# Eight additional tokens on fetched rows in place of sixteen, with low parts taken one product later and early row picks moved ahead of the scatter

## The chip, the cores and the metric

One core of one Trainium2 chip runs the whole program. The metric is device time in microseconds (us) of one launch. The kernel before took 2079.82 us in the median of three runs (2076.31 to 2084.03).

## The reference, cut to what matters

The program is two transformer blocks over 512 tokens of width 1024. The first block has attention and a convolution, then a mixture of 16,384 tiny experts ("PEER"); the second has sparse attention and a recurrence. The change touches the expert layer only:

```
s = einsum('chpd,hpnd->chpn', q, keys)       # 8 heads, two halves, 128 keys each
sv, si = top_k(s, 16)                        # per head and half
top_s, sel = top_k(sv0[:, None] + sv1[None, :], 16)
eidx = si0 * 128 + si1 at sel                # 8 x 16 = 128 experts for a token
g = softmax(top_s)
act = gelu(einsum('chkd,cd->chk', u_tab[eidx], xb))
out = einsum('chk,chkd->cd', g * act, v_tab[eidx])
```

So each token uses 128 rows of `u_tab` and 128 rows of `v_tab`, 1024 floats each.

## The kernel before, in words

**Two ways through the experts.** The first FETCH = 128 tokens take the reference's way: each sits on a partition, and an indirect DMA fetches one row per token, 512 KB a fetch, 128 fetches from u and 128 from v. The next EXTRA = 16 tokens take it too, laid out as 16 tokens by SHARED = 8 rows a fetch, so 16 fetches of u and 16 of v. For each fetched tile VectorE does one multiply with a sum (u) or one multiply and add (v) over 128x1024: a "pick". The other 512 - 128 - 16 = 368 tokens go densely: all 16,384 experts are multiplied with them, `gelu(u x)` is multiplied with a gate that is zero for experts not chosen, and the result is multiplied with v. `REST - EXTRA` = 368 is the number of columns of each of these matmuls.

**The dense way.** Every fp32 product is made of three fp32r matmuls: high weights with high data, high weights with low data, low weights with high data (L515 to L517, and L921 to L923). A weight tile is 128x1024 (512 KB), and gives 8 x 3 = 24 matmuls. For each tile SP starts the load `wraw` (ring of 4), ScalarE casts it to the high part `wh` (ring of 3), and GpSimd, or for every other tile VectorE, subtracts to get the low part `wl`. There are 16 groups of 8 tiles of u and 8 of v. The u products of nine groups ("spilled", 72 tiles) are made early, during routing, and their gelu is stored in DRAM (`a_scratch`); the u products of the seven others (56 tiles) are made in the expert loop, and all 128 v products too.

**Routing and scatter.** `drive_routing` is an order written out by hand that all engines follow. Routing of 128 tokens at a time is a chain of VectorE sorting steps. In its first two rounds the spilled products run beside it. Then three rounds of 128 tokens each turn the chosen gates into dense gate matrices: for four tokens (a "quad") VectorE builds one-hot tiles (`hots`), ScalarE weighs them, TensorE multiplies them. During these loops VectorE makes the first EARLY_PICKS = 42 picks, from three row buffers. GpSimd's `pick` issues the fetches: at its pick number m it issues rows up to m + 3, and waits for the pick that frees the buffer, all in order with its `wl` work.

**The expert loop** goes U(n+1, i+1), V(n, i), U(n+1, i+2), V(n, i+1) and so on. For U(n, i) VectorE multiplies gelu with the gate (L2421), ScalarE casts that to its high part WTH (L1652), VectorE waits for the cast and subtracts for WTL (L2424). For V(n, i) VectorE makes `wl` when it is its turn, waits for the product, adds it to h (L2436), and makes its picks. `fetch_schedule` deals the picks that are left (251) over the products. ScalarE casts the next weight tile in the same order as its WTH casts. Where the next group is spilled, no u product stands between two v products ("crowded" below); where it isn't, the loop is called "dense".

SP's queue holds the loads of weights, of gates, and of spilled tiles; before it loads a spilled tile it waits until WTH and WTL have been made from the tile five places earlier (L2985 to L2989).

Of the kernel before, what the change touches and what calls it, by code (L numbers as in the profile page):

```python
# [45 lines left out]
BLOCKS = REST // 32  # L46
EXTRA = 16
SHARED = 128 // EXTRA
# [94 lines left out]
def build_program(nc, hT, wstream, gains, consts, trig, w_uq, w_ukv, keys, w_uk, w_uv, w_rg, u_rows, v_rows, out):  # L143
# [1137 lines left out]
    def drive_routing(route, spill, spilled, scatter, pick, ahead=None):  # L1281

        for tt in range(2):
            steps = route(tt)
            for n in range(13):
                for _ in range(2):
                    next(steps, None)
                spill()
                if tt == 1 and n > 2:
                    pick()  # L1290
                if tt == 1 and n % 3 == 2:
                    spill()
            for _ in steps:
                pass
        picks = 10
        for tt in range(1, 4):
# [3 lines left out]
            for n in range(begin, 16):  # L1300
# [11 lines left out]
                scatter((tt - 1) * 128 + n * 8)  # L1312
                while picks < (10, 18, 26)[tt - 1] + (8, 8, 16)[tt - 1] * now // whole:
                    pick()
                    picks += 1
                while done < ROUTE_STEPS * now // (whole - 1):
                    next(steps, None)
                    done += 1
# [566 lines left out]
    def vector(dve):  # L1885
# [511 lines left out]
        def picks_after():  # L2397
            for _ in range(PICKS_AT[product_no[0]]):
                pick()
            product_no[0] += 1  # L2400


        dve.tensor_tensor(gg, gn[:, GCOL["g_fin"]:GCOL["g_fin"] + 8], gn[:, GCOL["g2"]:GCOL["g2"] + 8],
                          ALU.mult).then_inc(*scaled.tell("gg"))
        for what, n, i in EXPERTS:
            if what == "U":
# [14 lines left out]
                dve.tensor_tensor(u, u, gr[n % 2][:, :, i * 32:i * 32 + 32], ALU.mult).then_inc(*gated.tell((n, i)))  # L2421
                for x in ([i - 1] if n == 0 and 0 < i else []) + ([i] if n > 0 or i == 7 else []):
                    dve.wait_ge(*wt_hi.at(n, x))
# [8 lines left out]
            if n == N_GROUPS - 1 and i > 1:  # L2432
# [3 lines left out]
            dve.tensor_tensor(hx[i][:, FETCH + EXTRA:S], bank_of["V", n, i][:, EXTRA:REST], hx[i][:, FETCH + EXTRA:S],  # L2436
                              ALU.add).then_inc(*h_added.tell(("V", n, i)))
            picks_after()
            if (n, i) == (N_GROUPS - 2, 7):
# [260 lines left out]
    def gpsimd(pool):  # L2700
# [135 lines left out]
        def pick():  # L2836
            made[0] += 1
            fetch(min(made[0] + 3, EARLY_PICKS))

# [297 lines left out]
```

## Time and profile before

| what | us |
|---|---|
| median of three runs | 2079.82 |
| profiled execution, its own time | 2077.86 |
| its span in the trace | 2075.9 |
| TensorE matmul busy | 2025.1 |
| VectorE busy | 1475.7 |
| GpSimd busy | 1061.3 |
| ScalarE busy | 997.2 |

The page's first part gives busy time of each engine; matmuls are pipelined, and their recorded lengths overlap, so that two matmuls whose starts are 0.167 us apart each show 0.33 us. The rate of starts (the x of a stretch) tells more than the busy share. In the 40 slices VectorE stands at 8 or 9 tenths from about 830 us to 1450 us, and the DMA engines at 9 from about 730 us to 1450 us.

### The profile page before, as it was taken

Reading aid. Unit: us, or ns where it says so; the run is one execution under the profiler, and the core shown is the slowest. Engines: PE = TensorE matmul, PEld = TensorE weight load, DVE = VectorE, ACT = ScalarE, POOL = GpSimd, SP = SyncE. Lnnn points to the kernel's source line nnn. Section 1 sums busy time; section 2 is a strip of 40 time slices with the busy share of each in tenths; the row PEclk is TensorE's granted clock in tenths of the full one; section 3 lists DMA queues with packets and bytes.
Section 4 is the critical chain, followed back from the end, with each engine's and each line's share of the span. In section 5 each row is a group of like instructions: output and inputs, shape, how many; then the busy total and the mean of one; then the engine's idle time right before and its main releaser. Section 6 shows DMA issues by size and latency. Waiting matters only on the chain.

```text
span 2075.9 us, 31764 instructions
## 1 busy us (share of the span) xinstructions
PE 2025.1 (98%) x11815; PEld 1804.4 (87%) x11815; DVE 1475.7 (71%) x2840; ACT 997.2 (48%) x1825; POOL 1061.3 (51%) x615
## 2 busy tenths in 40 slices
PE   9999999999999999999999999999999999999998
PEld 8746889999999999999999999999967777877777
DVE  6247547979999478888888888887687535067763
ACT  4347433367789733333333333333546652356643
POOL 3222456864446577685667767684344444411242
PEclk9999999999999999999999999999999999999999
DMA  5330225776669899999999999996322223210021
GB/s 203 80 99 12 82 82 173 253 240 229 239 236 325 311 338 372 362 391 356 328 374 344 367 336 396 336 388 244 120 77 76 84 91 111 95 41 31 21 82 61
DMA packets 150935, 435.31 MB, mean 210 GB/s; under 512 B 14464, under 2 KB 61184, under 8 KB 148992
## 3 DMA queue, kind: packets, MB, share of 16 engines
q1 hardware_dynamic: 109312, 282.29, 39.1%
q0 software_dynamic: 41472, 151.01, 19.3%
q8 instruction: 95, 1.56, 0.3%
q14 instruction: 56, 0.46, 0.1%
HBM read 391.28 MB, written 41.97 MB: 209 GB/s over the span
## 4 chain that ended last, share of the span: by engine, by line
PE 76%; DVE 12%; DMA 4%; issue 4%; ACT 3%; POOL 2%; SPq 0%; DVEq 0%; ACTq 0%
PE bank L515 15%; PE bank L516 14%; PE bank L517 14%; PE bank L921 4%; PE bank L922 4%; PE bank L923 4%; DMA wraw<-in_wstream 4%; PE bank L902 3%; DVE wide L2390 2%; PE bank L1142 2%; PE bank L690 1%; DVE wl L1917 1%; DVE fetched L2370 1%; ACT WTH L1652 1%; POOL fetched L2830 1%
## 5 line engine op out<-in xcount | busy, mean ns | idle before, releaser
L2704 POOL TENSOR_TENSOR wl<-wraw,wh 128x1024 fp32r<-128x1024 f32 x272 | 678.8, 2500 | 716.7 <-ACT wh L1330 714.2
L1330 ACT CAST wh<-wraw 128x1024 fp32r<-128x1024 f32 x360 | 375.8, 1047 | 173.3 <-PE bank L517 118.3
L515 PE MATMUL bank<-WTH,wh 128*128 128x368 f32 x1024 | 340.4, 332 | 22.2 <-ACT wh L1330 11.3
L515 PE MATMUL bank<-XH,wh 128*128 128x368 f32 (+2 forms) x976 | 344.7, 353 | 3.0 <-issue 1.9
L516 PE MATMUL bank<-XL,wh 128*128 128x368 f32 (+2 forms) x976 | 340.8, 349 | 0.0
L517 PE MATMUL bank<-XH,wl 128*128 128x368 f32 (+2 forms) x976 | 339.5, 348 | 0.0
L516 PE MATMUL bank<-WTL,wh 128*128 128x368 f32 x1024 | 337.4, 330 | 0.0
L517 PE MATMUL bank<-WTH,wl 128*128 128x368 f32 x1024 | 337.2, 329 | 0.0
L515 PEld LDWEIGHTS bank<-WTH,wh 128*128 128x128 f32 x1024 | 192.8, 188 | 32.1 <-ACT wh L1330 21.4
L515 PEld LDWEIGHTS bank<-XH,wh 128*128 128x128 f32 x976 | 183.4, 188 | 25.7 <-issue 7.3
L921 PE MATMUL bank<-XH,wh 128*128 128x368 f32 x576 | 196.3, 341 | 7.1 <-ACT ijgT L1574 2.6
L516 PEld LDWEIGHTS bank<-XL,wh 128*128 128x128 f32 x976 | 183.2, 188 | 18.5 <-issue 2.2
L517 PEld LDWEIGHTS bank<-XH,wl 128*128 128x128 f32 x976 | 183.5, 188 | 16.4
L2830 POOL DMA_INDIRECT fetched<-in_u_rows,diag x144 | 158.0, 1097 | 69.0 <-DVE fetched L2370 41.2
L517 PEld LDWEIGHTS bank<-WTH,wl 128*128 128x128 f32 x1024 | 192.9, 188 | 0.0
L516 PEld LDWEIGHTS bank<-WTL,wh 128*128 128x128 f32 x1024 | 192.8, 188 | 0.0
L922 PE MATMUL bank<-XL,wh 128*128 128x368 f32 x576 | 191.7, 333 | 0.0
L923 PE MATMUL bank<-XH,wl 128*128 128x368 f32 x576 | 191.1, 332 | 0.0
L2830 POOL DMA_INDIRECT fetched<-in_v_rows,diag x144 | 161.5, 1122 | 42.9 <-issue 26.9
L2390 DVE SCALAR_TENSOR_TENSOR wide<-fetched,diag,wide 128x1024 f32<-128x1024 f32 x127 | 163.0, 1283 | 10.7 <-DMA fetched<-in_v_rows,diag 7.0
L1917 DVE TENSOR_TENSOR wl<-wraw,wh 128x1024 fp32r<-128x1024 f32 (+1 forms) x92 | 114.5, 1245 | 6.1 <-ACT wh L1330 5.2
L1652 ACT CAST WTH<-tmp 128x368 fp32r<-128x368 f32 x72 | 36.1, 501 | 171.8 <-DVE tmp L2421 149.2
(552 smaller groups left out, 3903.1 us busy)
## 6 DMA issues: line engine op xcount, KB each, us to landing
wraw<-in_wstream SPq DMA_DIRECT2D x360, 512.0 KB
g_scratch<-gs SPq DMA_DIRECT2D x12, 2048.0 KB
gr<-g_scratch SPq DMA_DIRECT2D x15, 1536.0 KB
a_scratch<-tmp SPq DMA_DIRECT2D x72, 184.0 KB
tmp<-a_scratch SPq DMA_DIRECT2D x46, 184.0 KB
sq<-a_scratch SPq DMA_DIRECT2D x26, 184.0 KB
shifted<-hc_scratch SPq DMA_DIRECT2D x12, 270.0 KB, 4.8
fetched<-in_u_rows,diag POOLq DMA_INDIRECT x144
```

The costliest lines, as they stand in the source:

```text
L515: pe.matmul(o, w1, x1, start=n == 0, stop=False)
L516: pe.matmul(o, w1, x2, start=False, stop=False)
L517: m = pe.matmul(o, w2, x1, start=False, stop=n == len(ks) - 1)
L902: mm = pe.matmul(bank[:, i * 128:i * 128 + 128], hots[q % 4][1][:, i, :], hots[q % 4][0][:, i, :], start=True, stop=True, skip_group_check ...
L921: pe.matmul(o, w1s[:, c:c + 128], XH[:, k, FETCH + EXTRA:S], start=k == 0, stop=False)
L922: pe.matmul(o, w1s[:, c:c + 128], XL[:, k, FETCH + EXTRA:S], start=False, stop=False)
L923: mm = pe.matmul(o, w2s[:, c:c + 128], XH[:, k, FETCH + EXTRA:S], start=False, stop=k == KT - 1)
L1330: act.copy(wh[n % NSPLIT][:, :], wraw[n % NRAW][:, :]).then_inc(*w_hi.tell(n))
L1917: return dve.tensor_tensor(lo, src, hi.bitcast(F32), ALU.subtract)
L2390: dve.scalar_tensor_tensor(wide[1][:, :], flat, eweight[:, s:s + 1], wide[1][:, :], ALU.mult, ALU.add).then_inc(*picked.tell(("v", s)))
L2704: return pool.tensor_tensor(lo, src, hi.bitcast(F32), ALU.subtract)
L2830: pool.indirect_dma_start(fetched[buf][:, :], None, u_rows if what in ("u", "u2") else v_rows, bass.IndirectOffsetOnAxis(ap=(eidx if what ...
```

## The change

EXTRA goes from 16 to 8 (SHARED from 8 to 16), so the dense matmuls have 376 columns in place of 368, there are 8 fetches less of u and 8 less of v, and the scatter has two quads more. VectorE's subtraction for WTL of groups 1 to 15 moves from U(n, i) to behind the addition to h of V(n-1, i-1) (both of the first two behind V(n-1, 0)). In the second routing round 14 picks are made in place of 10; the next two rounds of the scatter have 6 each in place of 8. Fetches are issued up to row m + 2 in place of m + 3. Routing steps beside the scatter end one iteration sooner.

```diff
--- before.py
+++ after.py
@@ -44,7 +44,7 @@
 FETCH = 128
 REST = S - FETCH
 BLOCKS = REST // 32
-EXTRA = 16
+EXTRA = 8
 SHARED = 128 // EXTRA
 EARLY_PICKS, LEAD, NEARLY, NFETCH = 42, 4, 3, 6
 NCAND = 80
@@ -1286,13 +1286,15 @@
                 for _ in range(2):
                     next(steps, None)
                 spill()
-                if tt == 1 and n > 2:
+                if tt == 1 and n > 1:
                     pick()
+                    if n in (8, 10, 12):
+                        pick()
                 if tt == 1 and n % 3 == 2:
                     spill()
             for _ in steps:
                 pass
-        picks = 10
+        picks = 14
         for tt in range(1, 4):
             steps = route(tt + 1) if tt < 3 else iter(())
             done = 0
@@ -1310,10 +1312,10 @@
                 if ahead:
                     ahead(KT * base + KT * count * now // whole)
                 scatter((tt - 1) * 128 + n * 8)
-                while picks < (10, 18, 26)[tt - 1] + (8, 8, 16)[tt - 1] * now // whole:
+                while picks < (14, 20, 26)[tt - 1] + (6, 6, 16)[tt - 1] * now // whole:
                     pick()
                     picks += 1
-                while done < ROUTE_STEPS * now // (whole - 1):
+                while done < min(ROUTE_STEPS, ROUTE_STEPS * now // (whole - 2)):
                     next(steps, None)
                     done += 1
 
@@ -2402,6 +2404,11 @@
 
         dve.tensor_tensor(gg, gn[:, GCOL["g_fin"]:GCOL["g_fin"] + 8], gn[:, GCOL["g2"]:GCOL["g2"] + 8],
                           ALU.mult).then_inc(*scaled.tell("gg"))
+        def low_part(n, x):
+            dve.wait_ge(*wt_hi.at(n, x))
+            minus_high(WTL[n % 2][:, x, EXTRA:], active(n, x)[:, EXTRA:],
+                       WTH[n % 2][:, x, EXTRA:]).then_inc(*wt_lo.tell((n, x)))
+
         for what, n, i in EXPERTS:
             if what == "U":
                 j = U_AT[n, i]
@@ -2419,7 +2426,7 @@
                 if n == 0 and i == 4:
                     dve.wait_ge(*ld_g[2].at("rest"))
                 dve.tensor_tensor(u, u, gr[n % 2][:, :, i * 32:i * 32 + 32], ALU.mult).then_inc(*gated.tell((n, i)))
-                for x in ([i - 1] if n == 0 and 0 < i else []) + ([i] if n > 0 or i == 7 else []):
+                for x in ([i - 1] if n == 0 and 0 < i else []) + ([i] if n == 0 and i == 7 else []):
                     dve.wait_ge(*wt_hi.at(n, x))
                     minus_high(WTL[n % 2][:, x, EXTRA:], active(n, x)[:, EXTRA:],
                                WTH[n % 2][:, x, EXTRA:]).then_inc(*wt_lo.tell((n, x)))
@@ -2435,6 +2442,9 @@
             dve.wait_ge(*gemm.at("V", n, i))
             dve.tensor_tensor(hx[i][:, FETCH + EXTRA:S], bank_of["V", n, i][:, EXTRA:REST], hx[i][:, FETCH + EXTRA:S],
                               ALU.add).then_inc(*h_added.tell(("V", n, i)))
+            if n + 1 < N_GROUPS:
+                for x in (0, 1) if i == 0 else (i + 1,) if i < 7 else ():
+                    low_part(n + 1, x)
             picks_after()
             if (n, i) == (N_GROUPS - 2, 7):
                 dve.wait_ge(*row_sum_mm.at("all"))
@@ -2835,7 +2845,7 @@
 
         def pick():
             made[0] += 1
-            fetch(min(made[0] + 3, EARLY_PICKS))
+            fetch(min(made[0] + 2, EARLY_PICKS))
 
         drive_routing(route, spill, spilled, scatter, pick)
 
```

## Rows read from the trace of the kernel before

**Rows 1.** The page, first part: busy time of each engine.

```profile
PE 2025.1 (98%) x11815; PEld 1804.4 (87%) x11815; DVE 1475.7 (71%) x2840; ACT 997.2 (48%) x1825; POOL 1061.3 (51%) x615
```

**Rows 2.** Windows: stretch, length, busy (count) of each engine, clock, DMA share, GB/s.

```profile
300.00:425.00 125.00, 123.81 (x767) 121.65 (x766) 102.46 (x446) 49.86 (x68) 91.52 (x41) 1.00 0.63 206
425.00:530.00 105.00, 98.19 (x648) 96.17 (x647) 92.61 (x267) 73.42 (x177) 52.77 (x27) 0.97 0.67 225
...
725.00:1430.00 705.00, 680.95 (x4019) 670.62 (x4018) 597.15 (x788) 248.18 (x340) 490.26 (x330) 1.00 0.97 360
```

**Rows 3.** The same view: the crowded stretches, last but one and the sum.

```profile
1280.00:1345.00 65.00, 60.22 (x353) 58.36 (x353) 56.17 (x69) 21.82 (x30) 39.49 (x26) 1.00 0.96 355
...
sum 273.00, PE 254.86 PEld 247.90 DVE 232.62 ACT 95.97 POOL 162.89; mean PE 36.41 PEld 35.41 DVE 33.23 ACT 13.71 POOL 23.27
```

**Rows 4.** The same view: the dense stretches, the last and the sum.

```profile
1345.00:1414.00 69.00, 69.00 (x415) 69.00 (x414) 60.99 (x68) 25.45 (x34) 54.14 (x39) 1.00 1.00 377
sum 419.00, PE 413.09 PEld 409.72 DVE 359.85 ACT 146.50 POOL 317.37; mean PE 68.85 PEld 68.29 DVE 59.98 ACT 24.42 POOL 52.90
```

**Rows 5.** Groups by shape, TensorE: count, busy us, mean ns, idle before.

```profile
L516 PE MATMUL bank<-WTL,wh 128*128 128x368 f32 x1024 | 337.4, 330 | 0.0
...
L922 PE MATMUL bank<-XL,wh 128*128 128x368 f32 x576 | 191.7, 333 | 0.0
...
L516 PE MATMUL bank<-XL,wh 128*128 128x512 f32 x384 | 151.8, 395 | 0.0
...
L516 PE MATMUL bank<-XL,wh 128*128 128x368 f32 x448 | 148.1, 331 | 0.0
...
L516 PE MATMUL bank<-XL,wh 128*128 128x264 f32 x144 | 40.9, 284 | 0.0
```

**Rows 6.** Waits from 725 to 1430 us: who for whom, total, times, longest.

```profile
ACT WTH L1652 <- DVE tmp L2421: 144.3, 53, 7.5
...
DVE WTL L1917 <- ACT WTH L1652: 64.2, 106, 3.0
...
ACT wh L1330 <- DMA wraw<-in_wstream: 24.5, 13, 3.9
```

**Rows 7.** VectorE in order of time, two products of a crowded stretch.

```profile
1299.37 1.12 DVE L2421 TENSOR_TENSOR tmp<-tmp,gr 128x384 f32<-128x384 f32 x1
1301.06 0.54 DVE L1917 TENSOR_TENSOR WTL<-tmp,WTH 128x368 fp32r<-128x368 f32 x1 [0.57 <-ACT WTH L1652]
1301.97 1.28 DVE L2390 SCALAR_TENSOR_TENSOR wide<-fetched,diag,wide 128x1024 f32<-128x1024 f32 x1
...
1307.51 1.12 DVE L2421 TENSOR_TENSOR sq<-sq,gr 128x384 f32<-128x384 f32 x1
```

**Rows 8.** The chain that ended last, 1010 to 1032 us: its longest piece.

```profile
1014.10 15.26 DMA wraw<-in_wstream
```

**Rows 9.** Groups by shape, VectorE: later u picks, then the 42 early ones.

```profile
L2370 DVE SCALAR_TENSOR_TENSOR fetched<-fetched,wide 128x1024 f32<-128x1024 f32 x86 | 102.8, 1214 | 10.3 <-DMA fetched<-in_u_rows,diag 9.8 <-issue 0.5
L2370 DVE SCALAR_TENSOR_TENSOR fetched<-fetched,below_XH 128x1024 f32<-128x1024 f32 x42 | 73.3, 1748 | 3.7 <-DMA fetched<-in_u_rows,diag 3.7
```

**Rows 10.** VectorE in order of time, second routing round to first one-hot tiles.

```profile
390.41 1.82 DVE L2370 SCALAR_TENSOR_TENSOR fetched<-fetched,below_XH 128x1024 f32<-128x1024 f32 x1 [2.21 <-DMA fetched<-in_u_rows,diag]
...
412.06 3.43 DVE L2370 SCALAR_TENSOR_TENSOR fetched<-fetched,below_XH 128x1024 f32<-128x1024 f32 x1
...
432.44 2.36 DVE L2327 TENSOR_TENSOR hots<-wide,ijgT 128x1024 f32<-128x1024 f32 x2 [5.55 <-ACT ijgT L1574]
...
435.85 1.28 DVE L2317 TENSOR_TENSOR sq<-wide,ijgT 128x512 f32<-128x512 f32 x2
```

**Rows 11.** GpSimd in order of time, the same stretch.

```profile
383.19 0.97 POOL L2830 DMA_INDIRECT fetched<-in_u_rows,diag  x1
...
410.78 6.98 POOL L2704 TENSOR_TENSOR wl<-wraw,wh 128x1024 fp32r<-128x1024 f32 x2
```

**Rows 12.** The chain that ended last: the scatter's matmuls for two quads.

```profile
529.93 1.78 PE bank L902 x16
```

## The prediction

> **What bounds the kernel now.** I read the page's first part first: TensorE is busy 98% of the span, VectorE 71%, GpSimd 51% [rows 1]. That makes TensorE the bound on average, so work added to it is paid in full wherever it doesn't idle. The windows then show where it does idle [rows 2]: 1.2 us of the 125 in the second routing round, 6.8 of 105 at the start of the scatter, 24 of 705 in the expert loop, where the DMA share is 0.97. I split the expert loop into the stretches in which the next group is spilled (crowded, 273 us) and the others (dense, 419 us), because the work per product differs. Crowded, TensorE idles 273 - 254.9 = 18.1 us [rows 3]; dense, 419 - 413.1 = 5.9 us [rows 4]. The reader is to see the rate as well: the crowded row has 353 matmuls in 65 us (0.184 us each), the dense one 415 in 69 us (0.166).
>
> Who sets the crowded pace? VectorE in order of time [rows 7]: from 1299.37 to 1307.51 it makes two products' share in 8.14 us, with no idle time but two waits of 0.57 us for ScalarE's cast WTH. TensorE would need 48 x 0.1666 = 8.0 us for two products. That pair has one pick a product; the schedule deals 83 picks to 72 crowded products, 1.15 each, so the mean pair takes 8.14 + 0.3 x 1.28 = 8.5 us, 0.5 more than TensorE's, and 36 pairs give 18 us: the same as the idle time of rows 3. The waits view agrees: VectorE waits 64 us for WTH in 106 places, and ScalarE 144 us (and more for the tiles named sq) for VectorE's gate product [rows 6], behind which ScalarE's next weight cast is queued. So in the crowded stretches TensorE follows VectorE. In the dense ones what is left looks like DMA: in the chain a weight load takes 15.26 us, just after a group's gates were asked for [rows 8], and ScalarE waits 24.5 us for weights in 13 places [rows 6].
>
> **The change part by part.** Everything is set against the profiled execution, 2077.86 us (span 2075.9 and 2 around it); the median of the runs is 2 us above it.
>
> *Columns.* 56 x 24 dense u matmuls, 72 x 24 spilled, 128 x 24 of v are 6144 (rows 5 show one third of each: 448, 576, 1024). Mean lengths are 330 to 333 ns at 368 columns, 395 at 512, 284 at 264 [rows 5]; their ends are modelled, but the differences follow the starts. Slopes are (395 - 331) / 144 = 0.444 and (331 - 284) / 104 = 0.452 ns a column. Eight columns are 3.56 ns, and 6144 of them 21.9 us. From below, a column per cycle of the 2.4 GHz level (the granted clock is 1.00 in nearly all windows) gives 20.5. I take 21.9, all on the path, as TensorE is the bound.
>
> The Trainium skill (TensorE: Matmul & The Clock Gate, Back-to-back issue gap) puts a sustained stream with weight loads at about 81 ns for 128 columns and 131 for 512, that is 0.13 ns a column; by that the columns would cost 6.4 us in place of 21.9. The rows contradict it with their 0.44 to 0.45.
>
> *Two more quads in the scatter.* Their matmuls take 1.78 us [rows 12], on TensorE's path: +1.8. VectorE pays two one-hot products of about 1.2 for one quad and 1.28 in two halves for the other [rows 10], 2.5 us, which the two picks taken out of that round give back (below).
>
> *Sixteen fetches less.* 16 x 1.28 = 20 us less of VectorE, 16 of GpSimd's issues of about 1 us, 8.4 MB less of DMA traffic, which at the loop's 360 GB/s [rows 2] is 23 us of a 705 us stretch. None of it is on TensorE; it counts only by what waits for it.
>
> *Low parts one product later.* VectorE now finds the cast finished and loses the 0.57 us [rows 7]. Its crowded pair becomes 8.5 - 1.14 - 0.1 (picks 1.10 a product in place of 1.15) = 7.3 us against TensorE's 48 x 0.170 = 8.17: it stops being the bound. What is late next: with the dense stretches' share of idle time (5.9 / 419), 3.8 us of the 18.1 stay for DMA, 14.3 go; a restart costs more than the idle time shows (in the crowded row 65 - 353 x 0.1663 = 6.3 us lost for 4.8 idle), so 14.3 x 1.3 = 18.6. I take -18. Bounds: 0 if something else holds the pace, and all the loop's losses, 24 x 1.3 = 31, if the dense ones go too. The new place adds a wait on no engine's path, I think: SP loads a spilled tile only when WTL of five places earlier is there, and the weight load is queued behind it; but that weight load needs the low part of a tile whose cast starts after the same v product (1.05 + 2.4 us later), while WTL follows that product by an addition and a subtraction, 1.1 us. V(n+1, 0) needs WTL of tile 7 last; it is made behind V(n, 6), with V(n, 7)'s 4 us in between.
>
> *Fourteen early picks ahead of the scatter.* Four more picks at a mean of 1.75 us [rows 9] are 7 us of VectorE before the first one-hot tile. There VectorE idles 5.55 us for TensorE's transposed gates [rows 10], and TensorE arrives there 30 x 24 x 3.56 ns = 2.6 us later than now: 8.1 us of cover. But rows are fetched late as well: today's fetch at 383.19 [rows 11] feeds the pick at 390.41, which waited 2.21 us for it [rows 10], and the same row is now picked one iteration (some 5 us) sooner, the later ones fetched one iteration later relative to their use. Where GpSimd's subtraction runs beside a pick, the pick takes 3.43 us and not 1.2 [rows 10, 11]. So the cover may fail by a little: I take +1, between 0 (covered) and 4 x 3.43 + 4 x 2.21 - 8.1 = 14 us.
>
> The Trainium skill (SBUF — State Buffer, Who interferes with whom) says that a VectorE instruction with two SBUF inputs contends with a GpSimd instruction that reads SBUF. The 3.43 us beside GpSimd's 6.98 us pair agree with it; by that rule all four new picks could be long, 4 x 3.43 = 13.7 us and 5.6 beyond the cover.
>
> *Start of the scatter.* From 425 to 530 us TensorE idles 6.8 us and the clock fell twice (mean 0.97) while VectorE is full [rows 2]. VectorE's work there stays (two picks out, one pair of quads in), TensorE's grows by 15 spilled tiles x 24 x 3.56 ns + 1.8 = 3.1 us: it fills idle time, -3. Bounds 0 and -8 (idle time and clock).
>
> *Fetches one row later.* GpSimd is not held up by VectorE before a subtraction; in the last round the slack of a row shrinks from some 3 us, but VectorE is at 0.8 there. 0, with +5 as the upper bound, one iteration.
>
> Sum: +21.9 + 1.8 - 18 + 1 - 3 = +3.7, 2081.6 for a profiled execution, and 2 more for the median: 2083.
>
> **The rivals.** (A) *Relief everywhere.* Less traffic and a freer VectorE let weight loads start earlier, so the DMA waits of the dense stretches go too. For it: 8.4 MB less, and loads wait for VectorE's low parts. Against: the 15 us loads come with a group's gates, which stay. -31 in the loop, -8 at the scatter: 23.7 - 39 = -15, 2065. (B) *Relief nowhere*, slower: the crowded pace is held by ScalarE's weight casts queued behind WTH or by DMA at 0.97 of its share, and the low parts' wait only moves. It decides if the rate of crowded stretches stays at 0.18 us a matmul. For it: DMA share; against: VectorE without a gap [rows 7] and ScalarE busy 96 of 273 us [rows 3]. +23.7 and nothing back: 2104. (C) *The early picks delay the scatter*: rows land late, VectorE reaches the first one-hot tile 5 to 14 us after TensorE; it decides once the cover of 8.1 us is gone. 2083 + 9 = 2092. (D) *Columns are cheap*: the matmul's pitch grows by about 1 ns and not 3.56; 2083 - 15.5 = 2067. Against it stand both slopes of rows 5. The rule of the Trainium skill cited above (TensorE: Matmul & The Clock Gate) would bring this about.
>
> **How the numbers follow.** Forecast 0.61 (its own range 2074 to 2092), A 0.14, B 0.13, C 0.10, D 0.02. The interval that leaves out 2 in 10: 2068 to 2097. A measurement tells 0.5% from no change, 10.4 us. Faster than 2069.4: most of A, D and a little of the forecast, 0.15. Slower than 2090.2: B, most of C, and a little of the forecast, 0.22. Same 0.63.
>
> **What would show it.** Right: mean length of a 376-column matmul 3.5 ns longer; VectorE's wait for WTH from 64 us to under 10, crowded stretches at 0.171 to 0.173 us a matmul, and VectorE with idle time in them for TensorE's products; dense ones hardly changed but for the columns; first one-hot tile at 434 to 437 us. Wrong: crowded stretches still at 0.18 (B), dense idle gone (A), the first one-hot tile after 440 us (C), the same matmul lengths (D).

## The result and the profile after

The changed kernel took 2082.03 us (median of 20 runs, 2078.88 to 2085.28), the kernel before 2076.64 in as many runs beside it (2069.63 to 2084.28, and one of 5131.72). The ratio is 1.0024 [1.0014, 1.0035]: 5 us slower, within the 0.5% called the same. The predicted 2083 and its 0.63 for "same" hold, though the forecast stood on a kernel before of 2079.82, 3.2 us above the 2076.64 measured here: as a difference it said +3.2, and the ratio gives +5.0 [2.9, 7.3]. The profiled execution has a span of 2083.0 us against 2075.9, which is 7.1 us more. The total came out right, but two terms behind it did not: TensorE pays 35 us for the eight columns and not 22, and its pauses shrink by 28 us and not by 20.

The page, first part, as [rows 1]. TensorE has 1% more of a longer span and hardly pauses; VectorE is busier by 22 us although it makes 16 picks less (part of why stands below), GpSimd less by 26.

```profile
PE 2056.5 (99%) x11831; PEld 1843.2 (88%) x11831; DVE 1497.5 (72%) x2819; ACT 999.9 (48%) x1835; POOL 1035.8 (50%) x599
```

The windows that answer to [rows 2], cut where the same work now lies: second routing round, start of the scatter, expert loop. In the last one TensorE was busy 681 us of 705; now it is 701.5.

```profile
300.00:425.00 125.00, 123.81 (x748) 121.67 (x747) 102.20 (x442) 46.73 (x64) 88.87 (x40) 1.00 0.62 203
425.00:535.00 110.00, 105.61 (x694) 103.58 (x693) 101.31 (x275) 80.18 (x191) 55.69 (x29) 0.98 0.65 223
...
735.00:1440.00 705.00, 701.49 (x4051) 700.20 (x4050) 613.19 (x773) 251.84 (x345) 457.91 (x315) 1.00 0.96 349
```

The crowded stretches, last but one and the sum of the seven, against [rows 3]. Idle time fell from 18.1 to 3.5 us. The seven rows count 1526 matmuls in 267 us, 0.175 each; the seven of before count 1501 in 273, 0.182.

```profile
1283.00:1349.00 66.00, 62.90 (x360) 61.93 (x360) 61.96 (x70) 22.27 (x31) 40.10 (x27) 1.00 0.95 346
...
sum 267.00, PE 263.49 PEld 262.24 DVE 254.31 ACT 99.43 POOL 162.25; mean PE 37.64 PEld 37.46 DVE 36.33 ACT 14.20 POOL 23.18
```

The dense stretches against [rows 4]: TensorE has no idle time left, where it had 5.9 us.

```profile
1349.00:1419.00 70.00, 70.00 (x406) 70.00 (x405) 61.00 (x63) 23.96 (x32) 46.31 (x35) 1.00 0.98 354
sum 420.00, PE 420.00 PEld 419.97 DVE 349.75 ACT 145.47 POOL 283.61; mean PE 70.00 PEld 69.99 DVE 58.29 ACT 24.24 POOL 47.27
```

The waits from 735 to 1440 us, against [rows 6]. VectorE's wait for the cast WTH is 1.8 us and was 64; it now waits for TensorE's products (46.0 us). ScalarE's wait for weights fell from 24.5 to 8.0 us, its wait for the gate product only from 144 to 137.

```profile
ACT WTH L1654 <- DVE tmp L2428: 137.2, 62, 6.7
...
DVE h L2443 <- PE bank L517: 46.0, 45, 2.7
...
ACT wh L1332 <- DMA wraw<-in_wstream: 8.0, 7, 3.5
...
DVE WTL L1919 <- ACT WTH L1654: 1.8, 4, 0.5
```

VectorE in order of time in the same crowded stretch, against [rows 7]: the low part (WTL) follows the addition to h with 0.1 us between, without the 0.57 us.

```profile
1305.64 0.53 DVE L2443 TENSOR_TENSOR h<-bank,h 128x376 f32<-128x376 f32 x1
1306.29 0.55 DVE L1919 TENSOR_TENSOR WTL<-tmp,WTH 128x376 fp32r<-128x376 f32 x1
1306.76 1.28 DVE L2392 SCALAR_TENSOR_TENSOR wide<-fetched,diag,wide 128x1024 f32<-128x1024 f32 x1
```

Something the prediction didn't count: in its new place the subtraction for WTL is longer. The first line is the kernel before, the second the changed one; the mean of one goes from 731 to 875 ns.

```profile
L1917 DVE TENSOR_TENSOR WTL<-tmp,WTH 128x368 fp32r<-128x368 f32 x72 | 52.6, 731 | 41.2 <-ACT WTH L1652 37.2 <-issue 4.0
L1919 DVE TENSOR_TENSOR WTL<-tmp,WTH 128x376 fp32r<-128x376 f32 x72 | 62.7, 875 | 3.6 <-ACT WTH L1654 1.8
```

Counted over all 128 of these subtractions, 10 took over 0.6 us before and 52 after (46 in low_later, below), and all but one of the long ones overlap a subtraction of GpSimd, where 3 of 118 short ones did before and 26 of 76 after. Their sum goes from 86 to 107 us (130 in low_later). In low_at_once, which has the old place, it is 87 us, so it is the new place in VectorE's order and not the columns.

VectorE ahead of the scatter, against [rows 10]. Three picks run one behind the other from 432.00 to 440, the first of them in 5.76 us (GpSimd subtracts beside it from 431.92 to 436.67; all 20 of the 42 early picks that took over 1.4 us overlap such a subtraction), and the first one-hot tile (below_XL here) comes at 439.99; in the kernel before the one-hot tiles began at 432.44.

```profile
391.00 3.19 DVE L2372 SCALAR_TENSOR_TENSOR fetched<-fetched,below_XH 128x1024 f32<-128x1024 f32 x1 [4.37 <-DMA fetched<-in_u_rows,diag]
...
432.00 5.76 DVE L2372 SCALAR_TENSOR_TENSOR fetched<-fetched,below_XH 128x1024 f32<-128x1024 f32 x1 [1.06 <-DMA fetched<-in_u_rows,diag]
...
438.84 0.08 DVE L2372 DVE_READ_ACCUMULATOR fetched<-fetched,below_XH 128x1 f32 x1
438.84 1.21 DVE L2372 SCALAR_TENSOR_TENSOR fetched<-fetched,below_XH 128x1024 f32<-128x1024 f32 x1
439.99 0.08 DVE L2372 DVE_READ_ACCUMULATOR fetched<-fetched,below_XH 128x1 f32 x1
439.99 1.21 DVE L2329 TENSOR_TENSOR below_XL<-wide,ijgT 128x1024 f32<-128x1024 f32 x1
```

**Phases, worked out from the start of every matmul.** Each cell: length of the phase in us / sum of TensorE's pauses in it, a pause being a distance between two starts above 0.4 us, less 0.17. The other three columns are the mean distance of two starts within products (distances under 0.24 us), in ns.

| kernel | routing | scatter | expert loop | tail | spilled u | dense u | v |
|---|---|---|---|---|---|---|---|
| before | 130.3 / 1.1 | 266.4 / 9.1 | 775.8 / 29.2 | 596.9 | 167.9 | 167.9 | 166.8 |
| after | 135.6 / 2.6 | 270.3 / 5.1 | 772.7 / 4.0 | 598.2 | 172.8 | 173.2 | 173.2 |
| low_later | 130.3 / 1.1 | 266.2 / 9.2 | 756.1 / 13.4 | 597.5 | 167.9 | 167.9 | 166.7 |
| fetches_only | 130.3 / 1.1 | 265.8 / 8.7 | 763.2 / 17.9 | 596.9 | 167.8 | 167.9 | 166.8 |
| columns_only | 134.0 / 1.1 | 271.0 / 8.5 | 781.7 / 12.0 | 597.9 | 172.8 | 173.2 | 173.2 |
| columns_384 | 136.4 / 1.1 | 271.0 / 8.5 | 787.9 / 13.1 | 597.3 | 175.5 | 175.4 | 173.8 |
| low_at_once | 136.1 / 3.1 | 270.5 / 4.9 | 776.6 / 7.1 | 598.3 | | | |
| early_undone | 134.0 / 1.1 | 268.6 / 6.3 | 769.1 / 0.8 | 597.1 | 172.8 | 173.2 | 173.2 |
| early_only | 136.8 / 5.2 | 266.6 / 7.6 | 771.4 / 26.3 | 597.3 | | | |
| sixteen | 134.4 / 4.1 | 265.4 / 7.3 | 758.2 / 14.2 | 597.0 | | | |
| low_steps | 130.3 / 1.1 | 274.3 / 14.3 | 763.2 / 19.1 | 597.4 | 167.9 | 167.8 | 166.7 |
| placed | 134.7 / 2.8 | 269.7 / 6.0 | 763.1 / 0.9 | 597.3 | 171.3 | 168.3 | 173.3 |
| v_at_0 | 134.0 / 1.1 | 268.6 / 6.1 | 768.8 / 0.8 | 598.4 | 172.8 | 172.5 | 173.3 |

The loop's pauses, split into crowded and dense stretches by whether dense u products are under 10 us apart (crowded / dense, us): before 22.1 / 7.0, low_later 12.2 / 1.2, fetches_only 12.7 / 5.3, columns_only 10.8 / 1.2, after 4.0 / 0.0.

Each row is one execution. That of low_later is the fastest of its runs (2058.68 us, median 2063.28), that of low_steps the slowest (2073.00, median 2067.86), so a few us between such rows need not come from the edit.

### The profile page after: what moved, and what is told of

Same layout as the page of the kernel before. It is cut to its first block, busy times and chain, and to the rows that moved or that the text cites. A ratio compares the mean times of both kernels' runs of the same rounds, so it can differ in the third digit from the quotient of the medians.

```text
span 2083.0 us, 31764 instructions
## 1 busy us (share of the span) xinstructions
PE 2056.5 (99%) x11831; PEld 1843.2 (88%) x11831; DVE 1497.5 (72%) x2819; ACT 999.9 (48%) x1835; POOL 1035.8 (50%) x599
## 4 chain that ended last, share of the span: by engine, by line
PE 88%; DVE 7%; DMA 2%; issue 1%; POOL 1%; ACT 1%; SPq 0%; DVEq 0%; ACTq 0%
PE bank L515 19%; PE bank L516 19%; PE bank L517 19%; PE bank L921 4%; PE bank L922 4%; PE bank L923 4%; PE bank L902 3%; PE bank L1142 2%; PE bank L690 1%; DMA wraw<-in_wstream 1%; PE wide L1165 1%; PE wide L1153 1%; PE bank L1165 1%; PE wide L648 1%; PE bank L784 1%
## 5 line engine op out<-in xcount | busy, mean ns | idle before, releaser
L1332 ACT CAST wh<-wraw 128x1024 fp32r<-128x1024 f32 x360 | 375.9, 1045 | 209.3 <-PE bank L517 173.3
L515 PE MATMUL bank<-XH,wh 128*128 128x376 f32 (+2 forms) x976 | 347.1, 356 | 1.1 <-ACT wh L1332 1.0
L515 PE MATMUL bank<-WTH,wh 128*128 128x376 f32 x1024 | 343.3, 335 | 3.5 <-issue 3.5
L517 PE MATMUL bank<-WTH,wl 128*128 128x376 f32 x1024 | 343.1, 335 | 0.0
L516 PE MATMUL bank<-WTL,wh 128*128 128x376 f32 x1024 | 343.0, 335 | 0.0
L516 PE MATMUL bank<-XL,wh 128*128 128x376 f32 (+2 forms) x976 | 343.0, 351 | 0.0
L517 PE MATMUL bank<-XH,wl 128*128 128x376 f32 (+2 forms) x976 | 342.1, 351 | 0.0
L515 PEld LDWEIGHTS bank<-XH,wh 128*128 128x128 f32 x976 | 183.4, 188 | 23.3 <-issue 3.9
L921 PE MATMUL bank<-XH,wh 128*128 128x376 f32 x576 | 197.8, 343 | 2.5 <-issue 2.4
L922 PE MATMUL bank<-XL,wh 128*128 128x376 f32 x576 | 193.2, 335 | 0.0
L923 PE MATMUL bank<-XH,wl 128*128 128x376 f32 x576 | 192.7, 335 | 0.0
L921 PEld LDWEIGHTS bank<-XH,wh 128*128 128x128 f32 x576 | 108.3, 188 | 5.5 <-issue 4.5
```

The costliest lines, as they stand in the source:

```text
L515: pe.matmul(o, w1, x1, start=n == 0, stop=False)
L516: pe.matmul(o, w1, x2, start=False, stop=False)
L517: m = pe.matmul(o, w2, x1, start=False, stop=n == len(ks) - 1)
L921: pe.matmul(o, w1s[:, c:c + 128], XH[:, k, FETCH + EXTRA:S], start=k == 0, stop=False)
L922: pe.matmul(o, w1s[:, c:c + 128], XL[:, k, FETCH + EXTRA:S], start=False, stop=False)
L923: mm = pe.matmul(o, w2s[:, c:c + 128], XH[:, k, FETCH + EXTRA:S], start=False, stop=k == KT - 1)
```

## The experiments

Each ratio is to the kernel before, timed on the same chip. To compare them, 0.1% is 2.08 us.

**low_later**: the kernel before, with the low parts later and nothing else of the change.

```diff
-                for x in ([i - 1] if n == 0 and 0 < i else []) + ([i] if n > 0 or i == 7 else []):
+                for x in ([i - 1] if n == 0 and 0 < i else []) + ([i] if n == 0 and i == 7 else []):
...
+            if n + 1 < N_GROUPS:
+                for x in (0, 1) if i == 0 else (i + 1,) if i < 7 else ():
+                    low_part(n + 1, x)
```

> The kernel before with one part of the change alone: the low parts of groups 1 to 15 are taken behind the addition of the v product before. Sixteen additional tokens, picks and fetches as before. Theory 1 (VectorE held the pace of the crowded stretches by its waits for the cast): its pair of products falls from 8.5 to 7.4 us, under TensorE's 8.0, the wait of VectorE for WTH falls from 64 us to under 10, gaps in the expert loop fall from 29 us to under 8, time -20 us (2056). Rival B (ScalarE's casts or DMA hold the pace): the wait disappears, the gaps stay, time within 3 us of before.

Measured: 2063.28 us, 0.9947 [0.9928, 0.9966], that is -11 us [-15, -7]; in the profiled execution -19. Its waits (725 to 1430 us) and its expert loop:

```profile
ACT wh L1330 <- DMA wraw<-in_wstream: 29.1, 21, 2.9
...
DVE WTL L1917 <- ACT WTH L1652: 7.6, 10, 3.0
```

```profile
725.00:1411.00 686.00, 674.86 (x4022) 670.36 (x4021) 639.10 (x789) 247.88 (x342) 475.87 (x331) 1.00 0.99 370
```

The wait for the cast goes and half of the loop's pauses with it, in the crowded stretches (22.1 to 12.2 us) and in the dense ones (7.0 to 1.2); in the crowded ones the rows of six windows have 1421 matmuls in 245 us, 0.172 each. So that wait did hold TensorE. Theory 1 has its sign and not its size: pauses of 13.4 us and not under 8, -11 us and not -20. What stays is the wait for weights, longer than before (29.1 us against 24.5), at a DMA share of 0.99.

**columns_only**: the kernel before with 376 dense columns; the additional tokens' gates are zero there, so the eight columns add nothing to the output.

```diff
+FIRST = 8
-        later = lambda name, *freed: ([(FETCH + EXTRA, S)], [name], [freed])
-        weighted = lambda name, *freed: ([(EXTRA, REST)], [name], [freed])
+        later = lambda name, *freed: ([(FETCH + FIRST, S)], [name], [freed])
+        weighted = lambda name, *freed: ([(FIRST, REST)], [name], [freed])
```

> The kernel before with 376 columns in the dense matmuls (tokens 8 to 15 of the additional sixteen go the dense way too, with gates of zero) and nothing else: fetches, picks, scatter and low parts as before. Theory 1 with the pitch seen in the changed kernel (5 ns more a matmul, 6144 of them): +31 us, less what the crowded stretches absorb, where TensorE's pair grows from 8.0 to 8.24 us under VectorE's 8.5: 36 x 0.24 = 9; +22 us (2098), and mean length of one matmul 335 ns. By the slope of the prediction (3.56 ns): +22 - 6 = +16 us and 333.5 ns. By the rule of the Trainium skill (TensorE: Matmul & The Clock Gate, Back-to-back issue gap), 1 ns a matmul, it would be +6 us; nothing else rests on this sentence.

Measured: 2093.16 us, 1.0085 [1.0065, 1.0106]: +17.7 us. The starts lie 4.9 to 6.4 ns further apart, and not 3.56; over 1728 spilled, 1344 dense u and 3072 v matmuls that is 8.5 + 7.1 + 19.7 = 35.3 us. It doesn't all reach the span, since the slower products give others time: the loop's pauses fall from 29.2 to 12.0 us with no other edit, and ScalarE's wait for weights (725 to 1430 us) from 24.5 to 10.4, though the wait for the cast is as long as it was and the traffic is no smaller. So the wait for weights is in part a consequence of TensorE's pace. Of the expected times both +22 and +16 lie in the interval [+13.5, +22]; the distance of the starts is theory 1's or more.

```profile
DVE WTL L1918 <- ACT WTH L1653: 70.0, 115, 3.1
...
ACT wh L1331 <- DMA wraw<-in_wstream: 10.4, 9, 2.8
```

**fetches_only**: the kernel before with eight additional tokens in all that fetches and picks (two more quads with it), the dense products still at 368 columns; tokens 136 to 143 are left out of the expert layer.

```diff
-EXTRA = 16
+EXTRA = 8
+FIRST = 16
...
-        weighted = lambda name, *freed: ([(EXTRA, REST)], [name], [freed])
+        weighted = lambda name, *freed: ([(FIRST, REST)], [name], [freed])
```

> The kernel before with eight additional tokens instead of sixteen in everything that handles fetched rows and picks (two more quads of routed work, 16 picks and half of the additional columns of each row's copy fewer), while the dense matmuls keep their 368 columns; tokens 136 to 143 are left out of the expert layer. What the expert layer gives back for the columns is measured alone. Theory (work on VectorE and the fetches keep TensorE in the crowded loop; less of it is quicker): the last expert loop loses 3 to 8 us and the whole is 0.996 to 0.999 of before (2067 to 2073). Rival (two more quads cost as much as the smaller row copies give): within 0.1% of before. Rival two, from the run with sixteen tokens against the change's own (the expert layer with eight was not seen to be any quicker): slower, 1.001 or more.

Measured: 2063.44 us, 0.9945 [0.9929, 0.9962], -11.4 us: more than the theory expected and against both rivals, and the clearest contradiction of the prediction, which gave the sixteen fetches nothing of their own. The first of the rows is the start of the scatter, where TensorE does 700 matmuls in 105 us (648 before, [rows 2]) and the clock no longer falls (1.00, was 0.97); the second is the expert loop. Of the lead at 530 us, 53 matmuls, 21 are left at 700 us: the whole scatter is only 0.6 us shorter, with two quads more in it, and the gain is the loop's (775.8 to 763.2 us), nearly all of it in the crowded stretches.

```profile
425.00:530.00 105.00, 102.06 (x700) 100.57 (x700) 93.30 (x269) 79.91 (x193) 52.38 (x27) 1.00 0.67 231
725.00:1417.00 692.00, 676.78 (x4017) 670.62 (x4016) 580.61 (x762) 247.98 (x341) 469.67 (x314) 1.00 0.96 354
```

In the waits of the same stretch the cast is again as before, and the weights are not:

```profile
DVE WTL L1918 <- ACT WTH L1653: 69.4, 120, 1.7
...
ACT wh L1331 <- DMA wraw<-in_wstream: 9.8, 10, 2.9
```

The fetches and the low parts' wait are thus two levers on the same pauses. By which way the fetches act is open: 8.4 MB less of traffic beside the weight loads, or 16 picks less on VectorE, whose order holds the crowded stretches. No run separates them, and the shorter wait for weights doesn't decide it, since columns_only has it too with all fetches in place.

**low_at_once**: the change without its low parts, which stay where they were.

```diff
-                for x in ([i - 1] if n == 0 and 0 < i else []) + ([i] if n == 0 and i == 7 else []):
+                for x in ([i - 1] if n == 0 and 0 < i else []) + ([i] if n > 0 or i == 7 else []):
```

> The changed kernel with the low parts back at their old place: eight additional tokens, early picks and fetches as changed. If the relief is set by the balance of the two engines, little is lost: VectorE's pair is 8.5 - 0.1 = 8.4 us against TensorE's 48 x 0.173 = 8.3, 36 x 0.1 = 4 us and some restarts: +5 us against the changed kernel (2087). If moving the low parts is what took all gaps away, whatever the columns: +18 to +25 us (2100 to 2107).

Measured: 2088.32 us, 1.0063 [1.0043, 1.0083]. So in the changed kernel the low parts are worth 8 us by the ratios (1.0063 to 1.0024) and 4.4 in the profiled spans, against 11 and 19 alone: 7.1 us of pauses were left in the loop, of which 3.1 went with them. That is the first expectation (+5) and not the second (+18 to +25).

**sixteen**: the change with sixteen additional tokens again, so without its columns and its saving of fetches.

```diff
-EXTRA = 8
+EXTRA = 16
```

> The changed kernel with sixteen additional tokens and not eight: low parts, early picks, fetches and routing steps as changed. Theory 1: 368 columns at the old pitch and VectorE off the pace, so low_later's gain and what the scatter's order brings (its gaps fell from 9 to 5 us, the routing's rose by 1.5): -20 - 3 = -23 us against before (2053). Rival: with 16 fetches more, VectorE and DMA are the pace again (dense pair 6.6 us of VectorE against 8.0), and it ends where the kernel before is, within 5 us.

Measured: 2062.84 us (2057.99 to 2065.22), 0.9937 [0.9918, 0.9956], faster than both kernels: 18 us by the ratios below the change, with sixteen fetches more. The expected -23 against before wasn't reached (-13 [-17, -9]), and the rival's "within 5 us" fails too. With low_later (0.9947) and fetches_only it stands for the same finding from another side: each of the other parts gains while the products stay at 368 columns.

**placed**: the change with its columns placed otherwise. Spilled u products take 376 columns from place 0, dense u products 368 from place 8 (the last eight tokens are left out of them), v products are untouched.

```diff
-        later = lambda name, *freed: ([(FETCH + EXTRA, S)], [name], [freed])
+        later = lambda name, *freed: ([(FETCH + EXTRA, S - 8)], [name], [freed])
...
-                    o, c = banks[b][:, EXTRA:REST], k * 128
-                    pe.matmul(o, w1s[:, c:c + 128], XH[:, k, FETCH + EXTRA:S], start=k == 0, stop=False)
+                    o, c = banks[b][:, 0:REST - EXTRA], k * 128
+                    pe.matmul(o, w1s[:, c:c + 128], XH[:, k, FETCH:S - EXTRA], start=k == 0, stop=False)
```

> The changed kernel with the dense matmuls' columns placed otherwise, to tell width from place; it leaves out part of the expert layer for the last eight tokens. Spilled u products: 376 columns from token 128 on into the bank's column 0 (a place that is a multiple of 16 columns). Dense u products: 368 columns from token 136 on into column 8. v products as in the changed kernel: 376 columns from column 8. Starts are 167.9 ns apart at 368 columns and place 16, 172.8 to 173.2 at 376 and place 8. If the place costs: spilled u near 170.9 (3.3 for the width alone), dense u near 170. If width alone does: spilled u stays at 172.8, dense u falls to 167.9. Time: by the place 1728 x 2 + 1344 x 3 ns = 7 us less than the changed kernel, by the width 1344 x 5.3 = 7 us less.

Measured: 2073.7 us, 0.9994 [0.9981, 1.0006], 6 us under the change, as both expectations had it. Dense u products of 368 columns start 168.3 ns apart at place 8, where they took 167.9 at place 16; spilled ones of 376 take 171.3 at place 0 and 172.8 at place 8. So each expectation holds for one product: dense u as the width alone has it (167.9), spilled u near the 170.9 of the place. The number makes most of the price, the place 1.5 ns in spilled u.

**columns_384**: columns_only with 384 columns from place 0.

```diff
-FIRST = 8
+FIRST = 0
```

> The kernel before with 384 dense columns (all of the sixteen additional tokens also go the dense way, with gates of zero), place 0. If an odd place made the 376 columns dear, the pitch here is 166.7 + 16 x 0.42 = 173.4 for v, hardly more than at 376, and the time is within 4 us of columns_only (2093, +0.9% against before). If each eight columns cost 5 to 6.4 ns, the pitch is 178 to 179 and the time +17 to +20 us over columns_only.

Measured: 2101.53 us, 1.0121 [1.0105, 1.0136], +25 us, 7 us over columns_only by the ratios where the first expectation had at most 4 and the second 17 to 20. Here v products start 173.8 ns apart, 0.6 more than with 376 columns (expected 173.4 or 178 to 179), dense u products 175.4, 2.2 more, spilled ones 175.5, 2.7 more. Over sixteen columns the slope is 0.44 (v) and 0.47 ns (u), as [rows 5] had it; over the first eight of them it is 0.8 and 0.66.

**v_at_0**: early_undone (below) with the v products' 376 columns from place 0 of the tiles and of the bank.

```diff
-        weighted = lambda name, *freed: ([(EXTRA, REST)], [name], [freed])
+        weighted = lambda name, *freed: ([(0, REST - EXTRA)], [name], [freed])
...
-            act.copy(WTH[n % 2][:, i, EXTRA:], active(n, i)[:, EXTRA:]).then_inc(*wt_hi.tell((n, i)))
+            act.copy(WTH[n % 2][:, i, 0:REST - EXTRA], active(n, i)[:, EXTRA:]).then_inc(*wt_hi.tell((n, i)))
```

> The version with the early part undone, with its V products' 376 columns read from column 0 of the weighted tiles and written from column 0 of the bank instead of from column 8; the same columns, the same work. Theory (the place, not the number of columns, makes a part of the price): V matmuls start 170 to 171 ns apart instead of 173.2, 3072 of them give 7 to 10 us, 2068 to 2071 where the version it starts from took 2077.6. Rival (376 columns cost 173 ns wherever they lie): no difference, 2077 to 2079.

Measured: 2076.92 us, 1.0007 [0.9994, 1.0019], where early_undone has 1.0013 [1.0004, 1.0022]: no difference told, and v still starts 173.3 ns apart. The rival holds: for v products the place costs nothing.

**widths**: columns_384 in which the v products of a group take one of eight ranges of columns, by the group's number; the columns beyond are left out of the result. There are 16 groups, so two stand for each range, and not the four that the expectation says.

```diff
+V_COLUMNS = [(0, 352), (0, 360), (0, 368), (0, 372), (0, 376), (0, 380), (0, 384), (16, 384)]
-        weighted = lambda name, *freed: ([(FIRST, REST)], [name], [freed])
+        weighted = lambda name, *freed: ([V_COLUMNS[name[1] % 8]], [name], [freed])
```

> The version with 384 dense columns, in which the V products of each expert take another number of columns, four experts each: 352, 360, 368, 372, 376, 380 and 384 columns from column 0, and 368 from column 16; the columns beyond are left out. Read from it is how far apart the V matmuls start. Theory from the runs at 368 (166.8 ns), 376 (173.2) and 384 (173.8): the price goes by steps of 16 columns, so 372, 376, 380 and 384 all stand at 173 to 174 ns, 360 and 368 at 166 to 167, 352 some 7 ns below that, and the place makes no difference. Rival: it goes by the column, 0.45 ns each, and 376 was high for another reason: 372, 376, 380 at 168.6, 170.3, 172.1.

TensorE in order of time, for six widths the first and the last of a run of the same line (every third matmul); the columns are start and length in us. The table's third column divides the distance of the two starts by the number of matmuls between them; the fourth is worked out from every start of that width.

```profile
750.51 0.33 PE L517 MATMUL bank<-WTH,wh 128*128 128x352 f32 x1
...
756.31 0.33 PE L517 MATMUL bank<-WTH,wh 128*128 128x352 f32 x1
```

```profile
838.86 0.32 PE L517 MATMUL bank<-WTH,wh 128*128 128x360 f32 x1
...
845.58 0.32 PE L517 MATMUL bank<-WTH,wh 128*128 128x360 f32 x1
```

```profile
850.03 0.33 PE L517 MATMUL bank<-WTH,wh 128*128 128x368 f32 x1
...
854.03 0.33 PE L517 MATMUL bank<-WTH,wh 128*128 128x368 f32 x1
```

```profile
951.16 0.33 PE L517 MATMUL bank<-WTH,wh 128*128 128x376 f32 x1
...
956.88 0.34 PE L517 MATMUL bank<-WTH,wh 128*128 128x376 f32 x1
```

```profile
984.76 0.33 PE L517 MATMUL bank<-WTH,wh 128*128 128x380 f32 x1
...
990.41 0.33 PE L517 MATMUL bank<-WTH,wh 128*128 128x380 f32 x1
```

```profile
1430.03 0.33 PE L517 MATMUL bank<-WTH,wh 128*128 128x384 f32 x1
...
1435.75 0.33 PE L517 MATMUL bank<-WTH,wh 128*128 128x384 f32 x1
```

| columns | these two rows | ns a matmul | mean of both groups, ns |
|---|---|---|---|
| 352 | 5.80 us / 36 | 161.1 | 161.9 |
| 360 | 6.72 / 42 | 160.0 | 162.6 |
| 368 | 4.00 / 24 | 166.7 | 166.6 |
| 372 | | | 169.9 |
| 376 | 5.72 / 33 | 173.3 | 173.3 |
| 380 | 5.65 / 33 | 171.2 | 171.2 |
| 384 | 5.72 / 33 | 173.3 | 174.0 |

Both expectations fall. There are no steps of 16 columns (372 and 380 lie between), and it isn't 0.45 ns a column either: 368 to 376 costs 6.7 ns, 0.83 a column, and 380 is 2 ns cheaper than 376, in both groups. So for v products 376 is a bad width, at place 0 as at place 8. It isn't so everywhere: spilled u products of 376 columns at place 0 (placed) start 171.3 ns apart, on the line from 167.9 (368) to 175.5 (384, columns_384). Why is open. (The run's own time, 2095.6 us, 1.0091 [1.006, 1.0121], mixes the widths.)

**early_undone**: the change with the picks, the fetches' lead and the routing steps as before.

```diff
-        picks = 14
+        picks = 10
...
-            fetch(min(made[0] + 2, EARLY_PICKS))
+            fetch(min(made[0] + 3, EARLY_PICKS))
```

> The changed kernel with picks, fetches and routing steps ordered as before: eight additional tokens and low parts later remain. By the changed trace (routing +5.3 us of which 3.8 are columns, gaps at the scatter 5 us and not 9) the early part is worth -4 + 1.5 = -2.5 us, so this is 2 to 3 us slower than the changed kernel (2085). Rival C, that the early picks cost more than they give: this is 2 us or more faster than the changed kernel (2080 or less).

Measured: 2077.61 us, 1.0013 [1.0004, 1.0022], 2.3 us quicker than the change by the ratios, whose intervals overlap, and 8.0 in the profiled spans. That is rival C's sign. VectorE reaches the first one-hot tile 4.2 us sooner than in the change and waits there again, for the gates:

```profile
435.76 1.22 DVE L2327 TENSOR_TENSOR below_XL<-wide,ijgT 128x1024 f32<-128x1024 f32 x1 [5.92 <-ACT ijgT L1574]
```

**early_only**: the kernel before with just that part (the diff above the other way round).

> The kernel before with 14 early picks, fetches one row later and routing steps ending sooner, nothing else. From the kernel with sixteen tokens, whose routing took 134.4 us and scatter 265.4 against 130.3 and 266.4 before: +3 us (2077). If the later fetches make up for it elsewhere: -2 us.

Measured: 2078.93 us, 1.0009 [0.9996, 1.0022]: +1.9 us, not told from nothing. The routing phase is 6.5 us longer (4.1 of it pauses), the loop 4.4 shorter. With early_undone it points the same way: this part costs some 2 us, and neither run by itself tells that from nothing.

**low_steps**: low_later, with the routing steps of a round ending one iteration sooner.

```diff
-                while done < ROUTE_STEPS * now // (whole - 1):
+                while done < min(ROUTE_STEPS, ROUTE_STEPS * now // (whole - 2)):
```

> The kernel before with the low parts one product later, and the routing steps issued so that the last of them comes one iteration sooner. Theory (a pick in the last routing round holds VectorE, which the scatter's first product waits for): the scatter starts 1 to 3 us sooner, 2060 to 2062 where the version without this took 2063.3. Rival (the routing steps crowd VectorE's other work in the spilled products instead): the same or up to 3 us more.

Measured: 2067.86 us, 0.996 [0.9944, 0.9976], not quicker than low_later (0.9947). The first one-hot tiles still wait for the transposed gates, which this doesn't touch, and the scatter starts no sooner (routing phase 130.3 us in both), so the theory falls by its mechanism. By time alone its 1 us isn't excluded; the rival's "the same or up to 3 us more" holds within the intervals.

```profile
432.06 2.36 DVE L2327 TENSOR_TENSOR hots<-wide,ijgT 128x1024 f32<-128x1024 f32 x2 [5.56 <-ACT ijgT L1574]
```

## Why the prediction was right, and where it was not

**The sum.** Predicted +3.7 us in a profiled execution, measured +7.1, and by the ratio +5.0. The terms that can be read from the phases: columns +35.3 (forecast +21.9); pauses of the loop -25.2 (forecast -18); pauses of the scatter -4.0 (-3); pauses of the routing phase +1.5 (+1); two quads +1.8 as forecast. That makes +9.4. Shorter stops, starts 0.24 to 0.4 us apart, less 0.17 each, give another -4.2 in the loop and -1.7 in the scatter, and the tail is 1.3 longer: +4.8, which leaves 2.3 us of the 7.1 unassigned. As the forecast's -18 was to hold such stops (its factor 1.3), it stands against -29.4: two errors, 13.4 us on the columns and 11.4 on the loop, cancel. That the total came so near is in that part luck.

**Columns: the mis-sized term.** "Eight columns are 3.56 ns, and 6144 of them 21.9 us." They are 4.9 to 6.4 ns and 35.3 us. The slopes were taken between widths over 100 columns apart, and the slope from 368 to 384 agrees with them; but in v products 376 lies well above the line between its neighbours (widths). "All on the path" fails too: of the 35.3 us 17.7 reach the time in columns_only, as 17 us of the loop's pauses go. The mean lengths, which the prediction named as the sign, are a weak one: 335 ns against 330 [rows 5] says 5, the starts say 6.4. Rival D goes the other way altogether. The rule of the Trainium skill that it leaned on (TensorE: Matmul & The Clock Gate, Back-to-back issue gap) has 0.13 ns a column; the traces differ from it, with 0.38 ns from 352 to 384 columns in v products and 0.44 to 0.45 between the widths of [rows 5].

**Low parts later.** The mechanism is shown: the wait went from 64 to 1.8 us, and alone the edit gives 11 us [7, 15] and takes 15.8 us of pauses. The forecast of 18 was high for the medians. One part of the reason was left out of "VectorE now finds the cast finished and loses the 0.57 us": the moved subtraction got longer beside GpSimd's, 44 us over all 128 in low_later, against 57 us of waiting saved. The step "its crowded pair stops being the bound" holds (VectorE waits 46 us for TensorE's products). The pace of 0.175 us lies above the forecast 0.171 to 0.173 by the columns' excess: 0.1666 + 0.0064 is 0.173 with no pause at all. Rival B, with 0.18, is out.

**Sixteen fetches less: the step that failed.** "None of it is on TensorE; it counts only by what waits for it", and then nothing was counted. ScalarE's 24.5 us of waits for weights [rows 6] and the DMA share of 0.97 [rows 2] were read, and left to the dense stretches as a rest that stays. fetches_only gives 11.4 us with this part alone, its wait for weights down to 9.8. The relief isn't where the prediction's DMA rest was, though: fetches_only takes 9.4 us of pauses in the crowded stretches and 1.7 in the dense ones. "Dense ones hardly changed" is wrong as well, their idle time went from 5.9 us to none, but low_later and columns_only each take 5.8 of the 7.0 us there. In the loop rival A's relief came (forecast -31, measured -29.4), though not in the total, since the columns ate it.

**Parts that share a gain.** Alone the parts measure +17.7 (columns), -11.0 (low parts), -11.4 (fetches, with the quads), +1.9 (early picks): -2.8 us. Together they measure +5.0. The 8 us between are counted twice: wider columns remove 17 us of the loop's pauses by making TensorE slower, and so do the low parts (16) and the fetches (11), but there are 29 in all. The times alone leave the 8 just clear of their noise (four parts with 3 to 4 us either way, measured on three chips); that the three reliefs add up to 44 us of 29 is what shows the overlap. The prediction priced the columns in full and took the pauses off once, under the low parts, and so didn't count them twice. It had not seen that the columns and the fetches draw on them too.

**Early picks.** Rival C's sign all but came: first one-hot tile at 439.99 us (its mark was 440) and not at 434 to 437, some fetches 4.37 and 1.06 us late, a pick of 5.76 us beside GpSimd's subtractions; over the 42 early picks VectorE waits 18.1 us for rows and not 3.7 [rows 9], and the mean pick takes 1.98 us and not 1.75. The cover of 8.1 us failed, as the prediction allowed, but the price was 2 us and not 9 (TensorE paused 1.5 us more in the routing phase; where VectorE's other lateness was absorbed no run shows). The rule of the Trainium skill that the prediction cited (SBUF — State Buffer, Who interferes with whom) agrees with that long pick. VectorE came to the one-hot tiles 4.2 us later than in early_undone (439.99 against 435.76), between the +1 taken and the 5.6 that the rule gave.

**Start of the scatter** and **fetches one row later.** Pauses -4.0 where -3 was expected, but not for the reason given, that TensorE's own growth fills its idle time: columns_only has only 0.6 us less of pauses there (9.1 to 8.5), early_undone 2.8. The later fetches weren't tried by themselves; together with the early picks they cost the 2 us.

## What to carry to other kernels

Before trading matmul columns for other work, measure the exact width: the distance between two starts is read from a timeline in two rows, and one kernel with several widths in it compares them, for the product and the place that it has them in. Where TensorE is 98% busy, its pauses are a fixed sum that each relief draws on, a slower TensorE too, so single gains don't add up; price the part that is paid in full first. Work that no one waits for can still have a price: here sixteen fetches and their picks were worth 11 us. And a wait that a move removes may come back in part as a longer instruction: look at the mean length of the moved one, not only at its wait.

## What the runs showed of the hardware

- Width and pace of fp32r matmuls with a weight load each (v products of widths, clock 1.00, mean of two groups): 162, 163, 167, 170, 173, 171, 174 ns for 352, 360, 368, 372, 376, 380, 384 columns. It isn't monotonic: 380 is 2 ns under 376.
- The same width has another pace in another place of the kernel: 360 columns 160.0 ns in one group of widths and 165.2 in the other, 376 columns 171.3 ns for spilled u at place 0 and 173.3 for v at place 0.
- Subtractions and picks of VectorE that run beside a subtraction of GpSimd are often several times longer: 5.76 us in place of 1.2 for a pick, up to 2.7 in place of 0.54 for WTL. Nearly all long ones overlap one (51 of 52 and 20 of 20 in the changed kernel), and not every one that overlaps is long.
- In the kernel before the clock stood at its lower level (1.2 GHz, a share of 0.5) for 3.4 us from 507.2 and again from 524.3 us, after pauses of TensorE (distances of 2.3 us between starts at 504.2, 1.4 at 513.7 and 3.0 at 521.2). In fetches_only it didn't fall there; the longest distance in that stretch is 2.0 us.
